# The order and the number of the first loads in a two-block transformer kernel

## What is computed

```
h    = concatenate([meta_tokens, x])            # (272, 2048)
hn   = rmsnorm(h, mix_norm_g)                   # h * rsqrt(mean(h*h) + eps) * g
proj = hn @ w_in                                # cq = 512 of its columns come first here
...
cq   = rmsnorm(cq, cq_g); q = cq @ w_q_up
...
h    = h + mix @ w_out
h    = h + conv_glu(rmsnorm(h, ffn_norm_g), ...)
```

## Time and profile before

| | us |
|---|---|
| median of 3 runs (2793.18 to 2794.66) | 2793.36 |
| the profiled execution | 2792.94 |
| its span | 2791.3 |
| TensorE busy in the span | 2769.5 |
| VectorE busy in the span | 1653.4 |
| ScalarE busy in the span | 1245.7 |

### The profile page before, as it was taken

The page is one execution under the profiler, slowest core; times in us unless marked ns, Lnnn a source line. Parts: engine busy times, 40 slices in busy tenths (PEclk is TensorE's granted clock), DMA queues, the critical chain, the costliest instruction groups (busy, mean ns, idle before and its releaser), DMA issues.

```text
span 2791.3 us, 58111 instructions
## 1 busy us (share of the span) xinstructions
PE 2769.5 (99%) x22890; PEld 2739.3 (98%) x22890; DVE 1653.4 (59%) x2213; ACT 1245.7 (45%) x1549; POOL 84.4 (3%) x123
## 2 busy tenths in 40 slices
PE   9999999999999999999999999999999999999998
PEld 9898999999999999999999999999999999999998
DVE  7667786666666455455556665555655555554444
ACT  6456654434343344434444564444443344443343
POOL 0000000000000000000114100000000000000000
PEclk9999999999999999999999999999999999999999
DMA  6433445555554555555554455555555555555555
GB/s 242 142 125 113 141 167 185 179 189 184 182 192 172 199 168 197 192 184 175 186 182 152 167 173 184 188 186 187 184 187 183 188 180 180 180 188 196 182 173 181
DMA packets 140124, 497.83 MB, mean 178 GB/s; under 512 B 16512, under 2 KB 18944, under 8 KB 140000
## 3 DMA queue, kind: packets, MB, share of 16 engines
q1 hardware_dynamic: 136976, 491.34, 51.3%
q0 software_dynamic: 3024, 4.66, 0.8%
HBM read 493.31 MB, written 2.62 MB: 178 GB/s over the span
## 4 chain that ended last, share of the span: by engine, by line
PE 95%; DVE 2%; ACT 1%; issue 0%; DVEq 0%; DMA 0%; ACTq 0%; SPq 0%
PE acc L1306 31%; PE acc L1308 30%; PE acc L1307 30%; DVE wlo L802 1%; PE aux L1359 1%; PE aux L1443 0%; PE aux L1441 0%; PE aux L1339 0%; ACT whi L456 0%; PE aux L1350 0%; PE aux L1449 0%; PE aux L1435 0%; DVE ss L829 0%; PE aux L1365 0%; PE aux L1556 0%
## 5 line engine op out<-in xcount | busy, mean ns | idle before, releaser
L802 DVE TENSOR_TENSOR wlo<-raw,whi 128x1024 fp32r<-128x1024 f32 x926 | 1120.7, 1228 | 812.1 <-ACT whi L456 808.0
L1306 PE MATMUL acc<-xh,whi 128*128 128x256 f32 (+3 forms) x4968 | 1411.2, 284 | 4.1 <-DVE qkv L822 2.2
L1308 PE MATMUL acc<-xh,wlo 128*128 128x256 f32 (+3 forms) x4968 | 1399.4, 282 | 0.0
L1307 PE MATMUL acc<-xl,whi 128*128 128x256 f32 (+3 forms) x4968 | 1396.6, 281 | 0.0
L456 ACT ACTIVATE whi<-raw 128x1024 fp32r<-128x1024 f32 x926 | 957.0, 1054 | 870.7 <-PE acc L1308 841.8
L1306 PEld LDWEIGHTS acc<-xh,whi 128*128 128x128 f32 (+1 forms) x4968 | 937.6, 189 | 10.3 <-issue 5.4
L1307 PEld LDWEIGHTS acc<-xl,whi 128*128 128x128 f32 (+1 forms) x4968 | 935.2, 188 | 0.4
L1308 PEld LDWEIGHTS acc<-xh,wlo 128*128 128x128 f32 (+1 forms) x4968 | 935.0, 188 | 0.0
L1306 PE MATMUL acc<-acth,whi 128*128 128x256 f32 x1408 | 396.3, 281 | 0.1
L1308 PE MATMUL acc<-acth,wlo 128*128 128x256 f32 x1408 | 395.7, 281 | 0.0
L1307 PE MATMUL acc<-actl,whi 128*128 128x256 f32 x1408 | 395.7, 281 | 0.0
(11 more groups left out here) (291 smaller groups left out, 2277.8 us busy)
## 6 DMA issues: line engine op xcount, KB each, us to landing
raw<-in_wts SPq DMA_DIRECT2D x928, 512.0 KB, 4.1
bias<-distances POOLq DMA_DIRECT2D x64, 32.0 KB, 3.4
out_T<-h SPq DMA_DIRECT2D x4, 512.0 KB, 3.5
bias<-in_na_bias POOLq DMA_DIRECT2D x8, 217.7 KB, 3.0
h<-in_hT SPq DMA_DIRECT2D x3, 544.0 KB, 4.1
h<-in_hT SPq DMA_DIRECT2D x2, 272.0 KB, 4.0
distances<-quads POOLq DMA_DIRECT2D x1, 512.0 KB, 12.4
vec<-in_vecs SPq DMA_DIRECT2D x1, 146.0 KB, 2.3
```

The costliest lines, as they stand in the source:

```text
L802: dve.tensor_tensor(wlo[:, slot_of(at, j), :], raw[:, slot_of(at, j), :], whi[:, slot_of(at, j), :].bitcast(F32), ALU.subtract).then_inc(l ...
L1306: pe.matmul(dst, hi, x_hi(kt), start=kt == 0, stop=False)
L1307: pe.matmul(dst, hi, x_lo(kt), start=False, stop=False)
L1308: last = pe.matmul(dst, lo, x_hi(kt), start=False, stop=kt == chunks * per_chunk - 1)
```

## The change

The five loads of `h` become eight of two blocks each (272 KB), and each quarter's second half has a semaphore of its own, for which ScalarE waits in the middle of the quarter. SP waits for earlier landings before it issues later loads. The order in which the data is asked for stays the same, but for chunk 2, which now comes between the halves of quarter 1.

```
-        h_half_landed = sem("h_half_landed")
+        h_half_landed = [sem(f"h_half_landed{q}") for q in range(4)]
...
             load_h(0, 0, 2)
             load(0, 0)
-            load_h(0, 2, 2, h_half_landed)
             sp.wait_ge(h_landed[0], 16)
+            load_h(0, 2, 2, h_half_landed[0])
+            sp.wait_ge(raw_landed[0], 16)
             load(1, 1)
-            load_h(1)
-            sp.wait_ge(raw_landed[0], 16)
+            sp.wait_ge(h_half_landed[0], 16)
+            load_h(1, 0, 2)
+            sp.wait_ge(raw_landed[1], 16)
             load(2, 2)
+            sp.wait_ge(h_landed[1], 16)
+            load_h(1, 2, 2, h_half_landed[1])
             load(3, 3)
-            sp.wait_ge(h_landed[1], 16)
-            load_h(2)
+            sp.wait_ge(raw_landed[2], 16)
+            load_h(2, 0, 2)
+            load_h(2, 2, 2, h_half_landed[2])
             sp.wait_ge(lo_ready, 1)
             load(4, 0)
             sp.wait_ge(h_landed[2], 16)
-            load_h(3)
+            load_h(3, 0, 2)
+            load_h(3, 2, 2, h_half_landed[3])
             sp.wait_ge(lo_ready, 2)
             load(5, 1)
             sp.wait_ge(lo_ready, 3)
...
                     if b == 2:
                         high_part(At(-AHEAD, 0), 0)
-                        act.wait_ge(h_half_landed, 16)
+                    if b % 4 == 2:
+                        act.wait_ge(h_half_landed[q], 16)
                     act.activation(xh[:, b, :], h[:, b, :], ACT.Copy, scale=vec[:, VEC["mix_g"] + b:VEC["mix_g"] + b + 1])\
                         .then_inc(xh_ready, 1)
```

## The result

| | before | after |
|---|---|---|
| median of 22 runs, us | 2793.96 (2793.05 to 2794.91) | 2798.18 (2796.77 to 2800.34) |
| profiled execution, us | 2792.94 | 2798.66 |
| its span, us | 2791.3 | 2797.0 |

The ratio is 1.0015, with a 95% interval from 1.0009 to 1.0021. So the kernel is slower by 4.2 us. That is inside the 0.2% band to which the prediction gave 0.94, but 1.6 us above the top of its range (2796.6) and far from its +0.65 us.

A forecast was written before the change was run, and what follows sets the result against it. The prediction took TensorE to bound most of the kernel and VectorE's work its opening. Only chunk 1's +0.65 us counted, all other terms 0: 2793.36 + 0.65 = 2794.0 us, range 2792.4 to 2796.6.

The forecast's parts named there:

- What bounds the opening, and that a shift of VectorE's end moves the kernel's end by as much: Opening to 31.07 us: VectorE's own work bounds it from 10.03, and moving its end moves the kernel's end equally.
- Loads are served in the order of issue, so holding back gives nothing: Opening loads: later ones take no bandwidth from earlier ones, so chunk 0 lands at 6.5 us either way.
- Second half of quarter 0, 0: Load of h issued at 4.12 us, landing at 7.3, hidden while ScalarE is busy with chunk 0: cost 0.
- Chunk 1, +0.65: Issued at chunk 0's landing, 6.5, takes 3.1, lands at 9.6 us; VectorE's row starts at 10.7: +0.65 us.
- Chunk 2, nothing more: Issued at 9.6, lands at 12.7, ready at 13.8 us as VectorE reaches it: nothing beyond the 0.65.
- Chunks 3 and 4, 0 with 1 us to spare: Chunk 3 lands near 14.9 us, chunk 4 near 17.6, before VectorE wants them: cost 0, about 1 us to spare.
- Chunk 5, 0 with 0.8 as the bound: Issued about 16.5, landed 20.3 us at 399 GB/s, cost 0; at 311 GB/s landed 22.1, a hole of 0.8.
- ScalarE's waits in the middle of a quarter, 0: Three waits for pieces landing at most 0.7 us after the first, covered by two blocks' work: cost 0, uncovered 0.7 each.
- Three more pieces, 0: Three more issues on SP, 3 x 0.44 = 1.3 us of its time, counted in the load times: no separate cost.
- The rival with their fixed parts in the open: Three added pieces each expose 1.8 us while ScalarE stands still: price 6.05 us, time 2799.4, chance 0.03.
- the crowded case: Awaited opening loads take nearer 4.79 than 3.1 us: chunk 1 +1.5 to +2.4, chunk 5 up to 0.8; chance 0.15.
- the signs that the prediction named for being wrong: Chunk 1 landing before 8.91 or after 11.3 us, VectorE still before chunks 2 or 5, or TensorE's clock falling in the opening.

The follow-up runs named there:

- hold_behind: The changed kernel with chunk 6, the constants and chunk 7 held back until chunk 5 has landed; 2797.79 us, ratio 1.0015 to the kernel before.
- no_waits: Eight pieces of h and no wait of SP for a landing, each load issued once its slot is free; 2793.76 us, ratio 0.9999 to the kernel before.
- after_again: The changed kernel measured once more, beside later runs on one chip; 2797.68 us, ratio 1.0013 to the kernel before.
- early_only: The changed kernel without the waits for chunk 2's landing and quarter 2's first half; 2796.11 us, ratio 1.0005 to the kernel before.
- waits_only: The changed kernel's waits, with quarters 1 to 3 of h loaded whole; 2798.58 us, ratio 1.0016 to the kernel before.
- no_raw2_whole: The changed kernel without the wait for chunk 2's landing ahead of quarter 2, quarters 1 to 3 loaded whole; 2797.93 us, ratio 1.0012.
- five_first: The changed kernel with chunk 5 issued ahead of the wait for quarter 2's first half and of quarter 3's pieces; 2796.55 us, ratio 1.0010.
- pieces_only: Eight pieces of h, with the waits of the kernel before; 2794.51 us, ratio 1.0001 to the kernel before.
- raw3_wait: The changed kernel with one wait more, quarter 2 issued only when chunk 3 has landed too; 2798.93 us, ratio 1.0017.
- one_under_way: Each load from the first piece of h to chunk 5 waits for the landing of the one ahead; 2817.21 us, ratio 1.0083 to the kernel before.

## Why the prediction was wrong, step by step

*What bounds the opening, and that a shift of VectorE's end moves the kernel's end by as much*: right. In all 16 profiles, the execution's time less the start of the sum is 2761.5 to 2762.7 us (before: 2792.94 - 31.21 = 2761.7), but for hold_behind with 2764.1; the last section shows what was different there.

*Loads are served in the order of issue, so holding back gives nothing*: in all 16 profiles the chunks and pieces of `h` of the first 40 us land in the order of issue, and holding back gave nothing for chunk 0 (no_waits). But that "a later load doesn't take bandwidth from an earlier one" isn't true to the byte. In hold_behind, with nothing issued behind chunk 5, 5.71 MB had moved by its landing. For the same loads it was 6.10 MB before and 6.51 in the changed kernel: 0.4 and 0.8 MB of loads issued behind chunk 5 had moved ahead of its end.

*Second half of quarter 0, 0*: right, it lands at 4.15 + 3.9 = 8.0, before chunk 0's rounding ends at 8.2.

*Chunk 1, +0.65*: it took 3.07 us, as forecast, and 3.1 to 3.4 in all profiles that hold it back. VectorE was 1.31 late there, half of it because chunk 0 landed at 7.13 and not 6.5, which varies from run to run. In isolation the step cost 0.8 in the profile and 1.1 in the medians.

*Chunk 2, nothing more*: wrong in one profile and nearly right in the other. It took 4.29 us in place of 3.1, a hole of 1.17; in after_again 3.36 and 0.23. With the same loads ahead (half a quarter), five more profiles have 3.2 to 3.3 and holes of 0.1 to 0.22, and early_only 3.8 and 0.70. So the 3.1 carried over well, and the hole of 1.17 is an outlier whose cause is open. Behind a whole quarter (waits_only, no_raw2_whole) it took 4.2 and 4.55.

*Chunks 3 and 4, 0 with 1 us to spare*: chunk 3 was forecast to land at 14.9 and landed at 16.73; VectorE, 2.55 us late itself, didn't notice. In after_again it landed at 17.64, and the hole was 0.85.

*Chunk 5, 0 with 0.8 as the bound*: this step failed, and it is the largest term. The forecast was an issue at 16.5 and 3.8 us to landing, 20.3. It was issued at 18.83, since quarter 2's first half landed at 17.96 and not 15.6, and took 6.73: 25.56. I had carried the line of bytes at 399 GB/s into a stretch where even the kernel before had 356, 330 and 311, and where the waits now leave 244, 254, 316 and 295. I set the 311 aside since it "includes time in which nothing was asked for". That was misread: before, chunk 6 was under way until 21.70, and chunk 7 from 17.11 to 24.82. The same chunk 5, with quarter 3 ahead of it, had taken 4.95 us before (14.54 to 19.48), and I gave it 3.8. The bound has a slip, too: 11.2 us of bytes from 10.9, where chunk 2's begin, end at 22.1, and the landing comes 0.6 later (as I had added elsewhere), so that 311 GB/s gives 22.7 and a hole of 1.4, not 0.8. Measured from chunk 2's issue (10.24) to chunk 5's landing, the 3.49 MB of my line came in 15.3 us, 228 GB/s; the engines moved 292 GB/s in that time, with the rest for loads issued ahead of chunk 2 and behind chunk 5. VectorE stood still for 2.34 us there (0.94 in after_again).

An estimate puts the 6.1 us by which chunk 5 landed later (25.56 against 19.48) together. In the first 15 us 3.26 MB moved in place of 4.62; at 306 GB/s, the mean of the two windows behind, the 1.36 MB are 4.4 us. The 0.41 MB more of later loads are 1.3. Together they make 5.7. So what the DMA engines didn't move while SP waited is the larger part, and it was in no term of the sum.

I also overlooked that SP issues quarter 3 ahead of chunk 5, although it is wanted after it: five_first puts that order at 0.7 us (2.8 against 3.5), in runs on two chips and not clear of their noise.

*ScalarE's waits in the middle of a quarter, 0*: this term failed too. The pieces of quarter 1 aren't issued together, since chunk 2 goes between them: the second landed 3.6 us after the first (5.2 in after_again), not "at most 0.7". In the first profile this was hidden, since ScalarE was held up by chunk 2 until 14.55; in after_again ScalarE stood still for 0.90 us.

*Three more pieces, 0*: right within the noise, pieces_only is +0.5 with an interval from -2.2 to +2.8. The rival with their fixed parts in the open was not what happened. The Trainium skill (DMA: Bandwidth & Descriptors, Bandwidth) advises transfers of 1 MiB or more; cutting 544 KB in two showed no cost here.

The result is nearest in size to the crowded case (+1.5 to +3.2, chance 0.15), but that would be luck: its main term, chunk 1 at nearer 4.79 us, didn't happen (3.1 to 3.4). Of the signs that the prediction named for being wrong, two came: VectorE stood still before chunks 2 and 5, and the granted clock fell.

What stays open: why the rate falls from 399 to 311 GB/s within the first 25 us although loads are under way, which the kernel before does too, without the new waits; and why one and the same load in one and the same program takes 4.6 us once and 6.1 another time (chunk 3), or 6.7 and 5.3 (chunk 5). DMA engines that drift apart, so that the slowest sets the landing, would fit; no view here tells one engine from another, and it wasn't tried.

## What to carry to other kernels

Waiting for one landing before issuing the next load puts up to its whole 3 us in the open, and gave nothing back here. Give the loads in the order in which they are wanted, and let only the free buffer hold them. When you price a chain of waits, count what the DMA engines don't move while they have nothing to do: those bytes stand ahead of every later load. Take the rate of the stretch in which the load falls, not the best one, and look up what the very same load took before. Then follow the chain to its last link. A delay that is small at each link is not small at the one that has to wait for all.

## What the runs showed of the hardware

TensorE's granted clock fell in the opening or just behind it in six of the 16 profiles: in three with a hole of 1.1 to 1.4 us before chunk 2 (the changed kernel's first profile, waits_only, no_raw2_whole), in raw3_wait, in hold_behind, and in one_under_way. In the changed kernel, two windows:

```profile
17.00:19.00 2.00, 1.26 (x10) 1.26 (x11) 2.00 (x5) 2.00 (x3) 0.00 (x0) 1.00 0.92 311
19.00:21.00 2.00, 2.00 (x12) 2.00 (x11) 1.85 (x4) 0.90 (x2) 0.00 (x0) 0.52 0.94 335
```

After TensorE had been idle for 1.91 us before 17.74, its clock stood at about half (0.52, the 1.2 GHz level) from 19 to 21 us, and was back at 1.00 by 23. The prediction had named this as a thing to look for, without a price. It cost nothing that can be seen: the chain passes through the load of chunk 5 at that time, and from the start of the sum on this execution took as long as after_again, which had 1.00 throughout (2762.5 us both). In after_again TensorE's pauses were as long as 1.59 us. One_under_way, with pauses of up to 4.7 us, was at 0.50 from 15 to 20 and from 35 to 40 us, among other stretches.

In hold_behind it did cost. There TensorE waited for 2.76 us ahead of the sum at 35.48, and the clock fell just behind it:

```profile
34.00:36.00 2.00, 0.52 (x3) 0.49 (x3) 1.55 (x3) 0.64 (x1) 0.00 (x0) 1.00 0.79 260
36.00:38.00 2.00, 2.00 (x12) 1.99 (x11) 1.94 (x3) 1.72 (x3) 0.00 (x0) 0.61 0.25 78
38.00:40.00 2.00, 2.00 (x12) 2.00 (x11) 0.65 (x2) 0.16 (x1) 0.00 (x0) 0.53 0.79 248
40.00:42.00 2.00, 2.00 (x18) 2.00 (x17) 1.59 (x4) 1.34 (x2) 0.00 (x0) 1.00 0.55 213
```

From 36.4 to 39.8 us its matmuls start 0.21 us apart, not 0.12, and the chain passes through them. By an estimate from these steps that is 1.5 us, and this is about what hold_behind has more than the changed kernel from the sum to the end (2764.1 against 2762.5). So one and the same fall of the clock is free while TensorE waits for loads, and is paid once TensorE holds the chain.
